# Three norm borders of a ten-block kernel: the next input formed as root times (y by both norm weights) plus a prepared product of x

## What is computed

```python
for l in range(2):                                  # first stack; the second has no norm on y
    h = swiglu(rmsnorm(x, g[0]), wg[l,0], wu[l,0], wd[l,0])
    x = x + 0.5 * rmsnorm(h, g[1])
    h = mixer(rmsnorm(x, g[2]))                     # l=0: convolution and sliding window (SWA), l=1: FOX
    x = x + rmsnorm(h, g[3])
    h = swiglu(rmsnorm(x, g[4]), wg[l,1], wu[l,1], wd[l,1])
    x = x + 0.5 * rmsnorm(h, g[5])
# rmsnorm(x, g) = x * rsqrt(mean(x*x) + 1e-6) * g
# swiglu(h, wg, wu, wd) = (silu(h @ wg) * (h @ wu)) @ wd,   wg, wu: 1024 x 2816
```

## Time and profile before

| | us |
|---|---|
| median of 3 runs | 1721.12 |
| lowest, highest | 1717.29, 1721.56 |
| the profiled execution, its time | 1721.92 |
| its span | 1720.2 |
| TensorE busy in it (93%) | 1603.6 |
| VectorE busy (61%) | 1050.3 |
| ScalarE busy (48%) | 821.7 |
| mean granted TensorE clock | 0.967 of full speed |

### The profile page before, as it was taken

The page is one execution under the profiler, slowest core; times in us unless marked ns, Lnnn a source line. Parts: engine busy times, 40 slices in busy tenths (PEclk is TensorE's granted clock), DMA queues, the critical chain, the costliest instruction groups (busy, mean ns, idle before and its releaser), DMA issues.

```text
span 1720.2 us, 24082 instructions
## 1 busy us (share of the span) xinstructions
PE 1603.6 (93%) x9380; PEld 1390.9 (81%) x9380; DVE 1050.3 (61%) x1243; ACT 821.7 (48%) x985; POOL 40.4 (2%) x62
## 2 busy tenths in 40 slices
PE   6999895899999999899899998978999999799998
PEld 5888794688888888789688887867888879688887
DVE  5566778666666566645566666455666663565665
ACT  4444544554446444534554445444544444554443
POOL 6000000000000000000000000000000000000000
PEclk9999996899999999999999999999999999899999
DMA  7565551265555555454265554535565654145552
GB/s 253 179 196 181 172 146 63 85 209 173 193 195 184 183 196 174 158 171 158 74 194 187 183 184 158 163 107 167 176 199 181 203 174 155 42 148 195 185 182 97
DMA packets 197253, 284.86 MB, mean 166 GB/s; under 512 B 8816, under 2 KB 149136, under 8 KB 197184
## 3 DMA queue, kind: packets, MB, share of 16 engines
q1 hardware_dynamic: 193488, 271.09, 48.2%
q0 software_dynamic: 3552, 12.28, 2.2%
q10 hardware_dynamic: 144, 0.52, 0.1%
HBM read 282.81 MB, written 1.05 MB: 165 GB/s over the span
## 4 chain that ended last, share of the span: by engine, by line
PE 84%; DVE 9%; ACT 5%; issue 2%; DMA 0%; DVEq 0%; POOL 0%; POOLq 0%; ACTq 0%
PE ps L1483 39%; PE ps L1554 21%; PE ps L1473 11%; PE ps L1557 11%; DVE mx L1169 2%; ACT shared L839 1%; DVE w_lo L979 1%; PE ps L1503 1%; DVE xt L1038 1%; DVE xn L1001 1%; ACT xt L662 1%; DVE shared L1404 1%; ACT w_hi L618 1%; PE ps L1747 1%; DMA gain<-in_norm_g_dram 0%
## 5 line engine op out<-in xcount | busy, mean ns | idle before, releaser
L979 DVE TENSOR_TENSOR w_lo<-raw,w_hi 128x2048 fp32r<-128x2048 f32 x257 | 587.9, 2292 | 395.1 <-ACT w_hi L618 395.1
L618 ACT CAST w_hi<-raw 128x2048 fp32r<-128x2048 f32 x257 | 488.8, 1905 | 138.3 <-PE ps L1483 67.7
L1554 PE MATMUL ps<-xt,w_hi 128*128 128x512 f32 x1536 | 418.2, 394 | 0.0
L1554 PEld LDWEIGHTS ps<-xt,w_hi 128*128 128x128 f32 x1536 | 265.9, 189 | 38.2
L1557 PEld LDWEIGHTS ps<-xt,w_lo 128*128 128x128 f32 x1536 | 235.5, 189 | 32.4
L1557 PE MATMUL ps<-xt,w_lo 128*128 128x256 f32 x1536 | 244.1, 281 | 0.0
L1483 PE MATMUL ps<-xt,w_hi 128*128 128x256 f32 x1600 | 228.3, 286 | 4.7 <-issue 2.4
L1483 PEld LDWEIGHTS ps<-xt,w_hi 128*128 128x128 f32 x1600 | 209.8, 194 | 6.7 <-issue 2.6
L1473 PE MATMUL ps<-w_hi,xt 128*128 128x512 f32 (+1 forms) x576 | 188.0, 410 | 25.3 <-DVE xt L1038 13.1
L1483 PE MATMUL ps<-w_hi,ht_hi 128*128 128x512 f32 x528 | 163.9, 391 | 0.0
L1483 PE MATMUL ps<-w_lo,ht_hi 128*128 128x512 f32 x528 | 163.2, 390 | 0.0
(11 more groups left out here) (203 smaller groups left out, 1240.3 us busy)
## 6 DMA issues: line engine op xcount, KB each, us to landing
raw<-in_ffn_w_gate_dram SPq DMA_DIRECT2D x132, 512.0 KB, 4.0
raw<-in_ffn_w_up_dram SPq DMA_DIRECT2D x132, 512.0 KB, 5.0
raw<-in_ffn_w_down_dram SPq DMA_DIRECT2D x132, 512.0 KB, 4.2
raw<-in_fox_w_in_dram SPq DMA_DIRECT2D x24, 512.0 KB, 4.6
raw<-in_a_w_in_dram SPq DMA_DIRECT2D x24, 512.0 KB, 4.4
raw<-in_w_kv_dram SPq DMA_DIRECT2D x16, 512.0 KB, 5.1
raw<-in_ab_w_in_dram SPq DMA_DIRECT2D x14, 512.0 KB, 4.7
gain<-in_norm_g_dram POOLq DMA_DIRECT2D x12, 512.0 KB, 4.0
```

Of the source, the lines that this page charges most:

```text
L618: nc.scalar.copy(w_hi[slot][:, :], raw[slot][:, :]).then_inc(hi_made, 1)
L979: nc.vector.tensor_tensor(w_lo[slot][:, :], raw[slot][:, :], w_hi[slot][:, :].bitcast(F32), ALU.subtract).then_inc(lo_made, 1)
L1554: nc.tensor.matmul(ps[:, GU_LOOP + b, :], w_hi[slot][:, col[b]], xt[:, kb, :], start=kb == 0, stop=False)
```

## The change

It concerns the borders whose `post` has a norm and whose next step is an FFN (`fused`). There are three: behind SWA's output (border A), between FFN 1 and FFN 2 (B) and behind FOX's output (C).

- `fuse_ready`, on VectorE: the product of the two norm weights (`gg`) and of x with the next norm's weight (`xg`), 128 x 1024 three times, into a tile (`mx`) that is free then. It stands behind the last low half in `out` (A, C) and behind chunk 1 of FFN 1 (B).
- `fused_xn`, per tile: xn = y * gg, which waits only for ScalarE's square to be through with y, then xn = root * xn + xg.
- `added_y`, per tile: y times root times weight into `xg` (L1001's work), then x plus that. It stands behind everything else of the border on VectorE, behind the low half of p+2.
- VectorE's order: tile 0, group 0's low half, low half of piece p+1, group 1's, tile 1, groups 2 and 3, low half of p+2, then x.
- ScalarE: groups 2 and 3 are copied ahead of x's mean squares, and the high half of p+2 ahead of them.
- TensorE: group 0 is turned inside the last product of y, group 1 behind it, groups 2 and 3 inside and behind the second quarter of `first_product`; `rows_between` moves from between the halves of `gate_up(p + 2)` to after the second k of its second half.

```diff
             s["out"] = steps[n + 1]
+        if s["kind"] == "pre":
+            s["fused"] = bool(n and s["defer"] and steps[n - 1]["g"] is not None)
+            if s["fused"]:
+                steps[n - 2]["fuse"] = s
         if s["kind"] == "proj" and steps[n - 1]["kind"] == "pre":
...
         sinks = sb("sinks", [P, 8])
+        xg = mx[:, 0:8, :].rearrange("p a b -> p (a b)").rearrange("p (t n) -> p t n", t=T)
+        gg = mx[:, 8:12, :].rearrange("p a b -> p (a b)")
         neg_sinks = sb("neg_sinks", [P, 4, 2])
...
         n_z_ln = []
+        n_y_squared = []
...
                                           accum_out=pssq[:, t:t + 1]))
+                n_y_squared.append(n_step)
                 eps = epst if s["scale"] == 1.0 else eps4t
...
                         turn(s, 0)
+                        if s["fused"]:
+                            turn(s, 1)
                         post_square(post, 1)
-                        turn(s, 1)
+                        if not s["fused"]:
+                            turn(s, 1)
+                        else:
+                            hi_upto(p + RING - 1)
+                            turn(s, 2, 3)
                     else:
...
                     pre_square(s, 0)
-                    turn(s, 2, 3)
+                    if not s["fused"]:
+                        turn(s, 2, 3)
                     hi_upto(p + RING - 1)
...
+            def fuse_ready(s):
+
+                g_post, g_pre = use_gain(s["post"]), use_gain(s)
+                link(nc.vector.tensor_tensor(gg[:, :], g_post[:, :], g_pre[:, :], ALU.mult))
+                for t in range(T):
+                    link(nc.vector.tensor_tensor(xg[:, t, :], x[:, t, :], g_pre[:, :], ALU.mult))
+
+            def fused_xn(s, t):
+
+                post = s["post"]
+                linked()
+                dve.wait_ge(act_step, n_y_squared[T * post["at_normed"] + t])
+                for half in range(2):
+                    link(nc.vector.tensor_tensor(half_cols(xn, t, half), ps[:, 2 * t + half, :],
+                                                 gg[:, half * 512:(half + 1) * 512], ALU.mult))
+                    dve.wait_ge(prstd_made, T * post["at_normed"] + t + 1)
+                    linked()
+                    nc.vector.scalar_tensor_tensor(out=half_cols(xn, t, half), in0=half_cols(xn, t, half),
+                                                   scalar=prstd[:, t:t + 1], in1=half_cols(xg, t, half),
+                                                   op0=ALU.mult, op1=ALU.add).then_inc(xn_made, 1)
+
+            def added_y(s, t):
+
+                post = s["post"]
+                g = use_gain(post)
+                for half in range(2):
+                    if t == 0 and half == 0:
+                        dve.wait_ge(xn_made, 4 * (s["at"] + 1))
+                    nc.vector.scalar_tensor_tensor(out=half_cols(xg, t, half), in0=ps[:, 2 * t + half, :],
+                                                   scalar=prstd[:, t:t + 1], in1=g[:, half * 512:(half + 1) * 512],
+                                                   op0=ALU.mult, op1=ALU.mult).then_inc(normed_y, 1)
+                for half in range(2):
+                    xh = half_cols(x, t, half)
+                    dve.wait_ge(normed_y, 4 * post["at_normed"] + 2 * t + half + 1)
+                    nc.vector.tensor_tensor(xh, xh, half_cols(xg, t, half), ALU.add).then_inc(x_added, 1)
+
             def norms(s):
...
-                if s["defer"]:
+                if s["fused"]:
+                    fused_xn(s, 0)
+                    turn(s, 0)
+                    lo_upto(p + 1)
+                    turn(s, 1)
+                    fused_xn(s, 1)
+                    turn(s, 2, 3)
+                    lo_upto(p + RING - 1)
+                    added_y(s, 0)
+                    added_y(s, 1)
+                elif s["defer"]:
                     both(0, 0)
...
                 chunk_(1, 1, banks=GU_BANKS[1])
+                if s.get("fuse"):
+                    fuse_ready(s["fuse"])
                 with dve.Fori(2, NC - 1, 2) as c:
...
                     lo_upto(s["piece"] + 4)
+                    if s.get("fuse"):
+                        fuse_ready(s["fuse"])
...
-            def half_product(o, p, half, t, ends=(0, KB - 1)):
+            def half_product(o, p, half, t, ends=(0, KB - 1), part=range(4)):
                 w = [v[p % RING] for v in (w_hi, w_lo)]
-                for k in range(4):
+                for k in part:
                     kb = 4 * half + k
...
                         split(p + half)
-                    ins = half_product(ps[:, banks[t], :], p + half, half, t)
+                    o = ps[:, banks[t], :]
+                    if pre["fused"] and g == 1:
+                        half_product(o, p + half, half, t, part=(0, 1))
+                        turn(pre, 2)
+                        half_product(o, p + half, half, t, part=(2, 3)).then_inc(gu_tile0, 1)
+                        turn(pre, 3)
+                        continue
+                    ins = half_product(o, p + half, half, t)
                     if t == 1:
...
-                def gate_up(q, more=0, banks=None, between=lambda: None):
+                def gate_up(q, more=0, banks=None, between=lambda: None, at=(0, 3)):
...
                                                (kb, b % 2) == (KB - 1, 1)) for b in (0, 2, 1, 3)], stands="w")
-                                continue
-                            for b in range(4):
-                                nc.tensor.matmul(ps[:, GU_LOOP + b, :], w_hi[slot][:, col[b]], xt[:, kb, :],
-                                                 start=kb == 0, stop=False)
-                            for b in range(4):
-                                ins = nc.tensor.matmul(ps[:, GU_LOOP + b, 0:S], w_lo[slot][:, col[b]],
-                                                       xt_hi[:, kb, :], start=False, stop=kb == KB - 1)
+                            else:
+                                for b in range(4):
+                                    nc.tensor.matmul(ps[:, GU_LOOP + b, :], w_hi[slot][:, col[b]], xt[:, kb, :],
+                                                     start=kb == 0, stop=False)
+                                for b in range(4):
+                                    ins = nc.tensor.matmul(ps[:, GU_LOOP + b, 0:S], w_lo[slot][:, col[b]],
+                                                           xt_hi[:, kb, :], start=False, stop=kb == KB - 1)
+                            if k < 3 and (half, k) == at:
+                                between()
                         ins.then_inc(piece_used, 1)
-                        if half == 0:
+                        if (half, 3) == at:
                             between()
...
                 first_product(s, GU_BANKS[0], True)
-                gate_up(p + 2, banks=GU_BANKS[1], between=rows_between)
+                fused = steps[steps.index(s) - 1]["fused"]
+                gate_up(p + 2, banks=GU_BANKS[1], between=rows_between, at=(1, 1) if fused else (0, 3))
                 pe.wait_ge(r_row_made, f + 1)
...
                 down_block(q + 1, 0, 1, 0)
+                if s.get("fuse"):
+                    turn(s["fuse"], 0)
                 down_block(q + 1, 1, 1, 0, stop=True).then_inc(piece_used, 1)
...
                         split(q + n)
-                    ins = half_product(ps[:, 2 * t + n, :], q + n, half, t, (None, 4 * half + 3))
+                    early = (0, 1) if (t, n) == (1, 1) and s.get("fuse") else ()
+                    if early:
+                        half_product(ps[:, 2 * t + n, :], q + n, half, t, (None, None), early)
+                        turn(s["fuse"], 0)
+                    ins = half_product(ps[:, 2 * t + n, :], q + n, half, t, (None, 4 * half + 3),
+                                       range(len(early), 4))
                     if t == 1:
...
                 k = s["kind"]
-                if k == "pre":
+                if k == "pre" and s["fused"]:
+                    turn(s, 1)
+                elif k == "pre":
                     turn(s, 0, 1)
```

## The result

| | us | ratio to before, 95% |
|---|---|---|
| before, median in the comparison | 1719.44 | |
| changed, median of 4 (1732.11 to 1735.47) | 1734.36 | 1.0084 [1.0069, 1.0099] |
| changed, the profiled execution | 1733.90, span 1732.2 | |
| changed, run once more (e10) | 1734.30 | 1.0087 [1.0073, 1.0101] |

The change costs 0.84%, 14.9 us. The forecast was 1733.4 us, 12.3 more than before; before's median in this comparison lies 1.7 us under the 1721.12 from which it was worked out.

The account below looks back on a forecast made before the run. TensorE, busy 93% of the span, bounds the kernel, so only its waits count. Border terms 3.1 + 3.1 + 1.2 plus 4.9 for the clock give 12.3 us slower: 1733.4 us, range 1726 to 1739.

Parts of the forecast that it names:

- second half of gate/up starts later: At each border, TensorE waits for late weight piece p+3: 2.25 us at A and C, 0.3 at B.
- rows moved behind the wait: Transposes and diagonal products, formerly ahead of gate/up's second half, now lie inside it: 0.88 us at each border.
- lost behind the pause: After TensorE's new wait at each border, matmuls run at the lower clock: 1.6 us lost each.
- Before xn: At the borders, shorter VectorE work makes xn early: tile-1 product ends 2.2 us early at A, 4.2 at B.
- After xn: x's late additions (5.2 us) push square, Silu and piece p+3; at A TensorE waits 5.4 us.
- the second square: Sign in ScalarE's order: the square stands some 8 us behind the last low half of xt instead of 3.
- The prepared products: Three 128x1024 VectorE products ahead of the borders, 1.2 us each, 3.4 us together, falling in idle time: priced at zero.
- The clock: TensorE's clock falls behind the new pause at all three borders: 1.6 us each, 4.9 together.
- the clock stays up: Rival: the clock does not fall at the three waits; +7.4 us, 1728.5 us; chance 0.15.
- every instruction counts: Rival: each instruction added to VectorE costs, +6.6 us per border, +19.8, 1740.9 us; chance 0.05.
- The faster case: Rival: piece p+3 is ready before TensorE ends gate/up's first half, so 8.6 us gained, 1712.5 us; chance 0.07.
- the early input: TensorE's turned input ready sooner at the borders: 2.2, 4.2 and 2.2 us, 8.6 us together.

Follow-up runs that it names:

- e10: The changed kernel itself run once more, on one chip with e9; 1734.30 us, 1.0087.
- e5: Changed kernel with 38 matmuls, results unread, put into TensorE's pause ahead of weight piece p+3 at the three borders; 1731.27 us, 1.0071.
- e8: Changed kernel with only ScalarE's high half of weight piece p+3 made early, VectorE's low half left behind Silu; 1735.19 us, 1.0089.
- e3: Changed kernel with the transposes of the hidden values (rows) back between the two halves of gate/up; 1734.53 us, 1.0089.
- e2: Changed kernel with both halves of weight piece p+3 split early, VectorE's low half ahead of the additions into x; 1724.89 us, 1.0032.
- e4: Changed kernel with only 8 of 512 columns of each half of y added into x at the three borders; 1723.74 us, 1.0024.
- e1: Changed kernel with weight piece p+3 split at the border, not behind Silu, its low half behind the additions into x; 1707.94 us, 0.9931.
- e7: e1 with the transposes of the hidden values (rows) back between the halves of gate/up; 1721.62 us, 1.0008.
- e6: Changed kernel's order on TensorE and ScalarE only, with the before kernel's VectorE arithmetic and no prepared products; 1720.33 us, 1.0004.
- e9: e1's kernel run again, over more rounds and on one chip with the changed kernel; 1710.56 us, 0.9949.

## Why the prediction was right

By the same marks as in the prediction, from the square of y at each border:

| term | forecast | measured |
|---|---|---|
| second half of gate/up starts later, A / B / C | 2.25 / 0.3 / 2.25 | 1.98 / 0.14 / 2.05 |
| rows moved behind the wait | 0.88 each | 0.88 each |
| lost behind the pause, in the forecast all low clock, A / B / C | 1.6 each | 2.36 / 2.25 / 1.85, of it 2.06 / 1.96 / 1.58 given back by e5 |
| sum | 12.3 | 13.3 |

The total came out closer than its terms: the delay was forecast 0.6 us too long over the three borders and the loss behind the pauses 1.6 too small, and before ran 1.7 us lower in the comparison than in the runs that I started from. That 1733.4 met 1734.36 is in part luck; the borders' 13.3 against 12.3 is the fair measure.

- *Before xn.* Right to 0.3 us. xn's halves came 2.8 and 4.2 us after the square's start at A (2.6 and 4.0 forecast), TensorE turned group 0 inside the last product without a wait, and the tile-1 product ended 2.5 us early at A. I had said 2.2. One row was read as the wrong tile: the 24 matmuls of 5.68 us at 346.81 are those of tile 1; those of tile 0 took 5.65, so the sum is untouched.
- *After xn.* The step on which the sign hangs, and right: eight instructions took 5.05 us (5.2), and from the second square to TensorE's start there were 8.04 (8.0). The pause was 5.4 us at all three borders, as forecast. One sign was misread: the second square stood 1.0 us behind the last low half of xt before, not 3, and stands 7.3 behind it now, near the 8 that I named.
- *The prepared products.* 1.22 us for 128x1024 (1.2), priced at zero. At C they ended at 865.74 and held the first product of y back to 865.78, 1.2 us behind the square; TensorE came to the transposes at 867.38 and found the half ready, done at 867.32. The zero held by 0.06 us there; at A the half was 1.1 us early. VectorE in time in the changed kernel, at border A's FFN, where they stand ahead of the FFN's own elementwise work; TensorE runs on through them without a wait:

```profile
383.91 1.22 DVE L1059 TENSOR_TENSOR mx<-gain 128x1024 f32<-128x1024 f32 x1
385.04 2.35 DVE L1061 TENSOR_TENSOR mx<-x_res,gain 128x1024 f32<-128x1024 f32 x2
387.31 1.28 DVE L1177 TENSOR_TENSOR shared<-ps,xn 128x512 f32<-128x512 f32 x2
```

- *The clock.* Right in kind, too small: 6.5 us for 4.9, or 5.6 if only what e5 gave back is counted. I had taken the row behind 3.71 us; here the stretch at 0.50 is longer. The length of the pause does not explain that: over the three borders 7.9 us were lost behind 4.4 to 4.5 us (e8) and 7.5 behind 2.5 us (e3), more than the 6.5 behind 5.4, and what sets the loss stays open. The Trainium skill, TensorE: Matmul & The Clock Gate, section HAM oscillation, has each burst behind a long wait begin cold. At the borders the changed kernel, e2 and e4 agree in kind, with 0.50 behind or soon behind every pause of 2.44 us and more, and e5 has 1.00 where the pause was filled. What I drew from that page, that several short pauses are cheaper than one long one, e3 does not bear out.
- *The rivals.* That the clock stays up fell with the profile of the changed kernel. That every instruction counts fell with e1, which has them all and is faster: the Trainium skill's advice in VectorE: DVE Perf Modes, section Rules for kernel authors, to keep the number of instructions small, says nothing of where they stand, and here the same 19 instructions cost 13 us or bring 9. The faster case fell in the change and came true in e1: the early input was real, as that rival said.

## What to carry to other kernels

When a value is made early by putting off work that another value needs, follow the second value as far as the first: here x's additions stood in front of the root, the root in front of Silu, and, by mere order in two queues, Silu in front of a weight piece that has nothing to do with either. The cure was not to undo the change but to take that piece out of the queue (two calls put elsewhere, from +0.8% to -0.5%). And price a new pause of TensorE above its length: at these borders pauses of 2.4 to 5.5 us cost 1.7 to 2.9 us more.

## What the runs showed of the hardware

- At the three borders the granted clock fell to 0.50 behind every pause of 2.44 to 2.52 us (three in e2, three in e4, each costing 1.7 to 1.8 us against e1 beyond the pause), and behind one of three pauses of 1.86 us (e7). Beyond the pause, 1.85 to 2.36 us were lost behind 5.4 us, 2.3 to 2.9 behind 4.4 to 4.5 us (e8) and 2.3 to 2.7 behind the second pause of e3, so the loss does not simply grow with the length. I had expected 1.5 us and less to be safe.
- That is no rule for all pauses of this length. One pause of 2.41 us, behind transposes late in the kernel, is in all twelve profiles: the clock fell behind it in eight and stayed up in four (e1, e2, e5, e6). e1 and e9 are the same kernel and differ in it, so nothing in the kernel decides this alone. TensorE in time and its busy time behind the pause, e1 and then e9:

```profile
1435.21 1.18 PE L1553 MATMUL ps<-xt,w_hi 128*128 128x256 f32 x8 [2.41 <-issue]
1435.21:1438.00 2.79, 2.79 (x23) 2.79 (x24) 2.11 (x1) 0.65 (x1) 0.00 (x0) 1.00 0.00 0
...
1430.10 1.87 PE L1553 MATMUL ps<-xt,w_hi 128*128 128x256 f32 x8 [2.41 <-issue]
1431.00:1433.00 2.00, 2.00 (x11) 2.00 (x11) 2.00 (x1) 0.00 (x0) 0.00 (x0) 0.50 0.00 0
```

- 1.1 us of matmuls between pauses of 1.87 and 2.46 us did not save the clock (e3); 4.7 us of matmuls with 0.88 us of pause left did (e5).
- Eight VectorE instructions of 8 columns still take 1.03 us together in a row (343.46 to 344.49 in e4), 0.13 us apiece; the other 0.5 us of the 0.63 us of a 512-column one is its columns.
